# Stick-breaking attention with queries on partitions: the product of the stay probabilities by a VectorE scan, the weights turned back on TensorE

## The chip, the core and the metric

One core of one Trainium2 chip runs one launch of one decoder layer. Its engines work side by side and meet at semaphores: TensorE (PE for its matmuls, PEld for its weight loads), VectorE (DVE), ScalarE (ACT), GpSimd (POOL) and SyncE (SP, which here only issues DMAs). TensorE has a granted clock; a value of 1.00 in a row is 2.4 GHz, 0.50 is 1.2 GHz. The metric is the device time of the launch in microseconds (us). The median of the three runs shown of the kernel before is 673.02 us.

## What is computed

A sequence of 512 tokens of width 1024 goes through one input projection, eight attention heads of 64 dimensions beside a short gated convolution over 512 channels, an output projection with LayerNorm, and a mixture of 32 experts (two per token) with a second LayerNorm. All is float32. The part that matters here is the attention:

```python
z = jnp.einsum('bhqd,bhkd->bhqk', qb, kb) * scale
causal = s_pos[None, :] < t_pos[:, None]
log_stay = jnp.where(causal, jax.nn.log_sigmoid(-z), 0.0)
log_stay_after = lax.cumsum(log_stay, axis=3, reverse=True) - log_stay
a = jnp.where(causal, jnp.exp(jax.nn.log_sigmoid(z) + log_stay_after), 0.0)
outs.append(jnp.einsum('bhqk,bhkd->bhqd', a.astype(vb.dtype), vb))
```

For query t and key s the weight is sigmoid(z_ts), times the product of 1 - sigmoid(z_tj) over the keys j that lie between s and t. Since 1 - sigmoid(z) = sigmoid(-z), the sum of logs can as well be a running product.

## The kernel before

Every engine has its own hand-written list of instructions, and semaphores join the lists. The launch has these stages: adaLN vectors (`ada`, 24 chunks of 256 columns of w_ada, 8 before the projection and 16 beside what follows, each summed on DVE into `acc_rows`), the projection of q, k and v, the attention stage with the convolution in it, the row broadcasts (L1170), the output projection (L1180) with LayerNorm and router, then the 32 experts, in 16 pairs.

The attention stage works head by head. Of the 16 blocks of 128 queries by 128 keys, the 10 on and below the diagonal are kept, so that one head has ZW = 1280 score columns. They lie in three PSUM banks (`zbank(h)`, even and odd heads in different banks), with the keys on the 128 partitions:

- `scores(h)` on PE: 7 matmuls over the 128 rows of `kT`, which hold two heads; `qz` is q with the other head's 64 rows zeroed.
- `softplus_tail(h)` on ACT: Abs, Exp and Ln of the whole bank, then `softplus(h)` on DVE (L733), a mask of the diagonal blocks on POOL (L419), and `suffix_sums(h)` on DVE.
- `later_keys(h)` on PE (L1141): 8 matmuls with a triangle of -1 or with all -1 add the sums over later keys to the scores in PSUM, 1280 + 768 columns.
- Exp on ACT (L584) makes the weights, POOL masks them again, and `attend(p)` on PE (L1132) multiplies them with v, for two heads at a time, 64 output partitions each. `scores(h + 2)` may start only when the Exp has read the bank.

Between these, PE runs the 12 convolution projections `conv_proj(n)` (L1119, 8 matmuls of 512 columns each). They share one PSUM bank (bank 6), so each waits until ACT (`cc`) or DVE (`cx`, `cb`) has read the one before. CONV_AT spreads them over the heads. DVE does four more `ada` chunks (20 to 23) behind heads 0 to 3.

SP loads all weights in one fixed order through a ring of 4 buffers `stage` of 1 MB. A load is issued when the buffer's last user is done; for an ada chunk that is DVE's `ada`, for a convolution weight it is the second `conv_proj` that reads it. Two lines tie the stage to its end on PE:

```python
            pe.wait_ge(ada_done, NADACH - (ADA1 - ADA_PE))
            pe.wait_ge(prob_done, NH)
```

Of the kernel before, what the change touches and what calls it, by code (L numbers as in the profile page):

```python
# [80 lines left out]
CONV_AT = [0, 2, 3, 5, 6, 8, 9, 11, 12]  # L81
NOWHERE = 1024
OVT = 256
DIAG, OFF0, OFF2, OFF1, ZW = 0, 512, 896, 1024, 1280


def layer_kernel(nc, x, c, w_ada, b_ada, w_in, conv_w, w_out, ln1_g, ln1_b, w_router_group,
# [3 lines left out]
    with ctx:  # L91
# [6 lines left out]
        def sem(name):  # L98
# [12 lines left out]
        qz = at("qz", [P, NH, T], PAIR1)  # L111
        kT = at("kT", [P, NF, T], PAIR1 + 16 * KB)
        v = at("v", [P, TC, DA], PAIR1 + 24 * KB)
        expo = [at(f"expo{n}", [P, ZW], o) for n, o in enumerate(
            (PAIR1 + 32 * KB, PAIR1 + 37 * KB, REST + 48 * KB, PAIR1 + 42 * KB))]
        acc_cols = at("acc_cols", [P, ADA_PE * CW], PAIR1 + 32 * KB)
        conv_rows = at("conv_rows", [P, P], PAIR1 + 42 * KB)
        suffix = [at(f"suffix{n}", [P, 3 * P], REST + 53 * KB + n * 1536) for n in range(2)]
# [4 lines left out]
        softp = [at(f"softp{n}", [P, ZW], PAIR2 + 32 * KB + n * 5 * KB) for n in range(2)]  # L123
# [31 lines left out]
        tri_neg = sm("tri_neg", [P, P])  # L155
        neg_ones = sm("neg_ones", [P, P])
# [81 lines left out]
        z_done, abs_done, exp_done, ln_done = sem("z_done"), sem("abs_done"), sem("exp_done"), sem("ln_done")  # L238
        sp_done, sp_masked, suf_done, tri_done = sem("sp_done"), sem("sp_masked"), sem("suf_done"), sem("tri_done")
        prob_done, prob_masked, av_done, av_ev = sem("prob_done"), sem("prob_masked"), sem("av_done"), sem("av_ev")  # L240
# [153 lines left out]
        def _(pool):  # L394
# [5 lines left out]
            g.memset(neg_ones[:], -1.0).then_inc(fills, 1)  # L400
# [5 lines left out]
            pool.wait_ge(fills, 6)  # L406
# [3 lines left out]
            g.affine_select(out=tri_neg[:], in_=neg_ones[:], compare_op=ALU.is_ge, fill=0.0, base=0,  # L410
                            pattern=[[-1, P]], channel_multiplier=1)
            g.affine_select(out=before[:], in_=ones_b[:], compare_op=ALU.is_gt, fill=0.0, base=0,
                            pattern=[[1, P]], channel_multiplier=-1)
            g.memset(qz[:], 0.0).then_inc(consts, 1)

            def mask(t):

                d = t[:, DIAG:DIAG + T].rearrange("p (j t) -> p j t", t=P)
                return g.affine_select(out=d, in_=d, compare_op=ALU.is_gt, fill=0.0, base=0,  # L419
                                       pattern=[[0, TC], [1, P]], channel_multiplier=-1)  # L420

            def mask_probs(h):
                pool.wait_ge(prob_done, h + 1)
                mask(expo[h % 4]).then_inc(prob_masked, 1)

            for h in range(NH):
                pool.wait_ge(sp_done, h + 1)
                mask(softp[h % 2]).then_inc(sp_masked, 1)
                if h > 0:
                    mask_probs(h - 1)  # L430
            mask_probs(NH - 1)
# [89 lines left out]
        def _(act):  # L521
            s = nc.scalar
            s.preload_act_table_set("natural_log_exp_and_others")
# [6 lines left out]
            s.activation(csil[:, 1], csil[:, 0], ACT.Exp, scale=-1.0).then_inc(exp_c, 1)  # L530
# [9 lines left out]
            act.wait_ge(consts, 2)  # L540
            for n in range(16):
                act.wait_ge(proj_done, n + 1)
                src = ps[:, n % 4]
                if n < 4:
                    s.mul(qz[0:HD, 2 * n], src[0:HD], HD ** -0.5)
                    s.mul(qz[HD:P, 2 * n + 1], src[HD:P], HD ** -0.5).then_inc(proj_ev, 1)
                elif n < 8:
                    s.copy(kT[:, n - 4], src).then_inc(proj_ev, 1)
                else:
                    half, i = divmod(n - 8, TC)  # L550
                    s.copy(v[:, i, w_cols(half)], src[:, 0:CW]).then_inc(proj_ev, 1)

            def softplus_tail(h):

                e = expo[h % 4]
                act.wait_ge(z_done, h + 1)
                if h >= 4:
                    act.wait_ge(av_done, (h - 4) // 2 + 1)
                s.activation(e[:], zbank(h), ACT.Abs).then_inc(abs_done, 1)
                act.wait_ge(abs_done, h + 1)  # L560
# [790 lines left out]
```

## Time and profile before

| | |
|---|---|
| median of 3 runs | 673.02 us (667.49 to 673.24) |
| the profiled execution's span | 662.9 us |
| PE busy in it | 544.0 us (82%) |
| DVE busy | 268.7 us (41%) |
| ACT busy | 112.9 us (17%) |
| POOL busy | 107.8 us (16%) |
| mean granted TensorE clock | 0.923 |
| DMA | 164.11 MB, mean 248 GB/s |

The span runs from the first to the last instruction of one profiled execution; the device time of a run holds some us more around it. The busy shares are averages over stages that have different limits, so the stage that the change touches is to be read by itself. The profile's chain of waits follows the work that ended last back to what released it. PE stands in it with 67% of the span, DMA with 15%, and SP's queue, DVE, ACT and POOL with 6, 5, 2 and 2%.

### The profile page before, as it was taken

Reading aid. Unit: us, or ns where it says so; the run is one execution under the profiler, and the core shown is the slowest. Engines: PE = TensorE matmul, PEld = TensorE weight load, DVE = VectorE, ACT = ScalarE, POOL = GpSimd, SP = SyncE. Lnnn points to the kernel's source line nnn. Section 1 sums busy time; section 2 is a strip of 40 time slices with the busy share of each in tenths; the row PEclk is TensorE's granted clock in tenths of the full one; section 3 lists DMA queues with packets and bytes.
Section 4 is the critical chain, followed back from the end, with each engine's and each line's share of the span. In section 5 each row is a group of like instructions: output and inputs, shape, how many; then the busy total and the mean of one; then the engine's idle time right before and its main releaser. Section 6 shows DMA issues by size and latency. Waiting matters only on the chain.

```text
span 662.9 us, 6931 instructions
## 1 busy us (share of the span) xinstructions
PE 544.0 (82%) x2665; PEld 311.8 (47%) x2665; DVE 268.7 (41%) x508; ACT 112.9 (17%) x172; POOL 107.8 (16%) x97
## 2 busy tenths in 40 slices
PE   0999999998889998989998169999997868888400
PEld 0984447854455454544455135555553434445100
DVE  4646566641554032224564762232232222221295
ACT  0111110125313233130112012112111111111010
POOL 3000000000000000004354421112112010100156
PEclk9979999999999999999998569999999998888755
DMA  8990777653034500029805439999999999999353
GB/s 298 312 290 8 249 251 249 195 191 127 0 128 160 221 0 1 0 100 423 364 33 216 196 95 395 419 414 416 418 417 417 418 418 418 418 417 380 113 194 127
DMA packets 67011, 164.11 MB, mean 248 GB/s; under 512 B 7560, under 2 KB 44460, under 8 KB 58796
## 3 DMA queue, kind: packets, MB, share of 16 engines
q1 hardware_dynamic: 58416, 149.96, 59.5%
q0 software_dynamic: 4608, 8.40, 3.5%
q10 hardware_dynamic: 3964, 5.44, 2.4%
q8 instruction: 15, 0.25, 0.2%
q14 instruction: 8, 0.07, 0.0%
HBM read 159.58 MB, written 12.58 MB: 260 GB/s over the span
## 4 chain that ended last, share of the span: by engine, by line
PE 67%; DMA 15%; SPq 6%; DVE 5%; ACT 2%; POOL 2%; issue 1%; POOLq 1%; DVEq 0%
PE ps L1119 13%; DMA w_gu<-in_w_up_dram 11%; PE ps L1245 11%; PE ps L1088 9%; PE ps L1180 8%; PE ps L1254 5%; PE ps L1095 4%; SPq L317 4%; PE ps L1141 4%; PE ps L1046 3%; DMA stage<-in_w_ada_dram 2%; PE ps L1238 2%; SPq L321 2%; PE ps L1132 1%; PE ps L1105 1%; ACT expo L584 1%
## 5 line engine op out<-in xcount | busy, mean ns | idle before, releaser
L1245 PE MATMUL ps<-w_gu,xT 128*64 128x256 f32 x1024 | 128.4, 408 | 22.8 <-DMA w_gu<-in_w_up_dram 19.7
L1245 PEld LDWEIGHTS ps<-w_gu,xT 128*64 128x64 f32 x1024 | 76.7, 146 | 65.0 <-issue 16.8
L1119 PE MATMUL ps<-hT,stage 128*128 128x512 f32 x192 | 84.7, 594 | 3.3 <-DVE u_conv L754 1.8
L970 DVE TENSOR_TENSOR ysb<-ps,rows_gate 64x512 f32<-64x512 f32 x64 | 44.1, 689 | 52.3 <-PE ps L1254 51.9
L1254 PE MATMUL ps<-w_dn,hidT 128*64 128x512 f32 x256 | 61.3, 599 | 0.4 <-ACT hidT L626 0.4
L962 DVE TENSOR_TENSOR hid<-ps,silu_sb 128x128 f32<-128x128 f32 x32 | 9.3, 292 | 123.4 <-ACT silu_sb L632 123.4
L1119 PEld LDWEIGHTS ps<-hT,stage 128*128 128x128 f32 x192 | 36.1, 190 | 47.0 <-issue 46.7
L1088 PE MATMUL ps<-hT,stage 128*128 128x512 f32 x128 | 57.1, 609 | 1.1 <-DVE hT L723 1.1
L707 DVE SCALAR_TENSOR_TENSOR acc_rows<-stage,csil,acc_rows 128x256 f32<-128x256 f32 x112 | 54.3, 485 | 4.0
L1180 PE MATMUL ps<-wo,mixT 128*128 128x512 f32 x128 | 55.4, 592 | 0.0
L460 POOL DMA_INDIRECT y_dram<-ysb,slot_row x16 | 16.1, 1008 | 201.9 <-DVE ysb L970 201.9
L419 POOL TENSOR_SCALAR_AFFINE_SELECT softp<-softp 128x512 f32<-128x512 f32 x8 | 5.1, 637 | 254.1 <-DVE softp L733 254.1
L1088 PEld LDWEIGHTS ps<-hT,stage 128*128 128x128 f32 x128 | 25.0, 197 | 32.5 <-issue 31.4
L1180 PEld LDWEIGHTS ps<-wo,mixT 128*128 128x128 f32 x128 | 24.2, 190 | 29.7 <-issue 29.7
L632 ACT ACTIVATE silu_sb<-ps 128x128 f32<-128x128 f32 x32 | 8.9, 278 | 139.7 <-PE ps L1245 139.7
L1254 PEld LDWEIGHTS ps<-w_dn,hidT 128*64 128x64 f32 x256 | 17.1, 136 | 23.8 <-issue 20.9
L1095 PE MATMUL ps<-stage,hT 128*128 128x256 f32 x128 | 27.8, 379 | 0.0
L1046 PE MATMUL ps<-csil,stage 128*128 128x1 f32 x96 | 18.1, 319 | 11.7 <-DMA stage<-in_w_ada_dram 11.7
L1095 PEld LDWEIGHTS ps<-stage,hT 128*128 128x128 f32 x128 | 24.3, 190 | 3.7 <-issue 0.5
L733 DVE SCALAR_TENSOR_TENSOR softp<-ps,expo 128x1280 f32<-128x1280 f32 x8 | 11.9, 1486 | 33.7 <-ACT expo L563 33.7
L1046 PEld LDWEIGHTS ps<-csil,stage 128*128 128x128 f32 x96 | 18.2, 291 | 11.8 <-issue 11.8
L1238 PE MATMUL ps<-ident,xg 128*128 128x128 f32 x128 | 18.4, 289 | 5.7 <-DMA xg<-h_dram,slot_tok 5.7
(197 smaller groups left out, 558.0 us busy)
## 6 DMA issues: line engine op xcount, KB each, us to landing
w_gu<-in_w_gate_dram SPq DMA_DIRECT2D x32, 1024.0 KB, 20.4
w_gu<-in_w_up_dram SPq DMA_DIRECT2D x32, 1024.0 KB, 23.5
w_dn<-in_w_down_dram SPq DMA_DIRECT2D x32, 1024.0 KB, 24.0
stage<-in_w_ada_dram SPq DMA_DIRECT2D x24, 1024.0 KB, 8.0
stage<-in_w_in_dram SPq DMA_DIRECT2D x12, 1024.0 KB, 9.0
wo<-in_w_out_dram SPq DMA_DIRECT2D x1, 4096.0 KB, 17.4
y_tok<-y_dram SPq DMA_DIRECT2D x8, 512.0 KB, 7.5
xs<-in_x_dram ACTq DMA_DIRECT2D x1, 2048.0 KB, 14.0
```

What stands on the lines that cost most here:

```text
L317: sp.dma_start(w_gu[u][e][:, g], src).then_inc(ld_gu[u][e], 16)
L707: link(w.scalar_tensor_tensor(out=acc, in0=st[:, k], scalar=csil[:, 3, k:k + 1], in1=acc, op0=ALU.mult, op1=ALU.add))
L970: ins = w.tensor_tensor(ysb[u][e * HD:(e + 1) * HD, b * 512:(b + 1) * 512], ps[b * HD:(b + 1) * HD, 6 + e, :], gate2r[b * HD:(b + 1) * HD, ...
L1046: t.matmul(col, st[:, k, f * P:(f + 1) * P], csil[:, 3, k:k + 1], start=k == 0, stop=False)
L1088: ins = t.matmul(dst, st[:, k, f * P:(f + 1) * P], hT[:, k], start=k == 0, stop=k == KC - 1)
L1095: ins = t.matmul(dst[:, 0:CW], hT[:, k, i * P:(i + 1) * P], st[:, k], start=k == 0, stop=k == KC - 1)
L1119: ins = t.matmul(ps[:, 6], st[:, k, (f % 2) * P:(f % 2 + 1) * P], hT[:, k], start=k == 0, stop=k == KC - 1)
L1141: add = lambda to, m, r, stop=False: t.matmul(to, m, r, start=False, stop=stop, skip_group_check=True)
L1180: ins = t.matmul(ps[:, 4 + 2 * (i % 2) + n], mixT[:, k, i * P:(i + 1) * P], wo[:, k, n * 512:(n + 1) * 512], start=k == 0, stop=k == KC - 1)
L1238: ins = t.transpose(flat[:, k * P:(k + 1) * P], xg[u][:, k * P:(k + 1) * P], ident[:])
L1245: ins = t.matmul(ps[a * SLOTS:(a + 1) * SLOTS, 2 + e, 0:2 * P], xT[u][:, k, e * SLOTS:(e + 1) * SLOTS], w_gu[slot][e][:, :, k, a * P:(a + ...
L1254: ins = t.matmul(ps[b * SLOTS:(b + 1) * SLOTS, 6 + e, :], hidT[e][:, a * SLOTS:(a + 1) * SLOTS], w_dn[slot][e][:, a, b * 512:(b + 1) * 512 ...
```

## The change

The scores come out with the queries on the partitions. One `scores(p)` serves the two heads of a pair: for each query block, the 64 rows of one head in `qT` are the stationary operand and its 64 rows in `kT` the moving one, first for the even head (rows 0 to 63) and then for the odd one (rows 64 to 127), into different banks. ACT takes sigmoid(-z) into `stay` and sigmoid(z) into `prob`. POOL masks the diagonal blocks of both, each in two instructions. DVE runs one scan over `stay` from the last column to the first, a product which `block_end` (a bf16 row of zeros, with a one at the last key of each query block) sets back to 1, and multiplies `prob` by it. PE turns the 10 blocks of `prob` back with transposes (`turn_probs`) into the same banks, ACT copies them to `probT` (`probs_out`), and `attend(p)` needs 8 matmuls instead of 14. `later_keys`, the softplus and the suffix sums are gone. The convolution projections now stand three to a pair, and `ada(20 + p)` stands behind the third of each pair. ACT loads another table at the start and one more (for an Exp of 16 columns) ahead of the router's softmax.

```diff
-            def suffix_sums(h):
-                f, sx = softp[h % 2], suffix[h % 2]
...
+            def weights_of(h):
+                st = stay[h % 2]
+                dve.wait_ge(stay_masked, 2 * h + 2)
+                w.tensor_tensor_scan(out=st[:, 0:ZW][:, ::-1], data0=st[:, 0:ZW][:, ::-1], data1=block_end[:, ::-1],
+                                     initial=1.0, op0=ALU.mult, op1=ALU.max).then_inc(scan_done, 1)
+                dve.wait_ge(scan_done, h + 1)
+                dve.wait_ge(take_masked, 2 * h + 2)
+                w.tensor_tensor(prob[h % 2][:], prob[h % 2][:], st[:, 1:ZW + 1], ALU.mult).then_inc(prob_done, 1)
...
-            for h in range(NH):
-                softplus(h)
-                suffix_sums(h)
-                for n in range(CONV_AT[h], CONV_AT[h + 1]):
-                    conv(n)
-                if 20 + h < NADACH:
-                    ada(20 + h)
+            dve.wait_ge(consts, 8)
+            for p in range(NPH):
+                weights_of(2 * p)
+                conv(3 * p)
+                weights_of(2 * p + 1)
+                conv(3 * p + 1)
+                conv(3 * p + 2)
+                ada(20 + p)
...
+            def sigmoids(h):
+                act.wait_ge(z_done, h // 2 + 1)
+                if h >= 2:
+                    act.wait_ge(prob_done, h - 1)
+                s.activation(stay[h % 2][:, 0:ZW], zbank(h), ACT.Sigmoid, scale=-1.0).then_inc(stay_done, 1)
+                if h >= 2:
+                    act.wait_ge(probt_done, h - 1)
+                s.activation(prob[h % 2][:], zbank(h), ACT.Sigmoid).then_inc(take_done, 1)
...
+            def probs_out(h):
+                act.wait_ge(probt_done, h + 1)
+                if h >= 2:
+                    act.wait_ge(av_done, h // 2)
+                s.copy(probT[h % 2][:], zbank(h)).then_inc(probt_ev, 1)
...
+            for p in range(NPH):
+                sigmoids(2 * p)
+                sigmoids(2 * p + 1)
+                if p > 0:
+                    av_out(p - 1)
+                conv_cc(3 * p)
+                probs_out(2 * p)
+                conv_cc(3 * p + 1)
+                probs_out(2 * p + 1)
+                conv_cc(3 * p + 2)
+            av_out(NPH - 1)
...
+            def scores(p):
+                if p > 0:
+                    pe.wait_ge(probt_ev, 2 * p)
+                for i in (3, 2, 0, 1):
+                    for h in (2 * p, 2 * p + 1):
+                        b = (h % 2) * HD
+                        ins = t.matmul(zbank(h)[:, QROW[i]:QROW[i] + (i + 1) * P], qT[b:b + HD, p, i * P:(i + 1) * P],
+                                       kT[b:b + HD, p, 0:(i + 1) * P], start=True, stop=True, skip_group_check=True)
+                ins.then_inc(z_done, 1)
+
+            def turn_probs(h):
+                pe.wait_ge(prob_done, h + 1)
+                z, a = zbank(h), prob[h % 2]
                 for j in range(TC):
...
+                    for i in range(j, TC):
+                        ins = t.transpose(z[:, KROW[j] + (i - j) * P:KROW[j] + (i - j + 1) * P],
+                                          a[:, QROW[i] + j * P:QROW[i] + (j + 1) * P], ident[:])
+                ins.then_inc(probt_done, 1)
...
+            for p in range(NPH):
+                scores(p)
+                if p > 0:
+                    attend(p - 1)
+                conv_proj(3 * p)
+                turn_probs(2 * p)
+                conv_proj(3 * p + 1)
+                turn_probs(2 * p + 1)
+                conv_proj(3 * p + 2)
+            attend(NPH - 1)
...
             pe.wait_ge(ada_done, NADACH - (ADA1 - ADA_PE))
-            pe.wait_ge(prob_done, NH)
+            pe.wait_ge(probt_ev, NH)
```

On PE the kernel before has these rows for one head in the steady part of the stage, from the scores of a head over one convolution projection to the sums over later keys of the head before it (a name's number is a buffer; `x8` is eight such instructions):

```order
L1105 MATMUL ps<-qz,kT 128x128 x4
L1107 MATMUL ps<-qz,kT 128x384
L1108 MATMUL ps<-qz,kT 128x128
L1109 MATMUL ps<-qz,kT 128x256
L1119 MATMUL ps<-hT,stage_63 128x512 x8
L1141 MATMUL ps<-softp_81,tri_neg 128x512 x2
L1141 MATMUL ps<-softp_81,tri_neg 128x256
L1141 MATMUL ps<-softp_81,neg_ones 128x128
L1141 MATMUL ps<-suffix_76,neg_ones 128x256
L1141 MATMUL ps<-softp_81,neg_ones 128x128 x2
L1141 MATMUL ps<-suffix_76,neg_ones 128x128
```

The changed kernel has these for a whole pair of heads, with 8 `attend` matmuls (left out here) behind the scores:

```order
L1107 MATMUL ps<-kT,qT 128x512 x2
L1107 MATMUL ps<-kT,qT 128x384 x2
L1107 MATMUL ps<-kT,qT 128x128 x2
L1107 MATMUL ps<-kT,qT 128x256 x2
...
L1127 MATMUL ps<-hT,stage_61 128x512 x8
L1116 MATMUL ps<-ident,prob_79 128x128 x10
L1127 MATMUL ps<-hT,stage_63 128x512 x8
L1116 MATMUL ps<-ident,prob_80 128x128 x10
L1127 MATMUL ps<-hT,stage_63 128x512 x8
```

So every piece of attention work on PE now has a convolution projection on both sides, and nothing of it comes twice in a row but scores and `attend`.

On DVE the kernel before ends the stage like this (the last two heads, then the row work):

```order
L733 SCALAR_TENSOR_TENSOR softp_81<-ps,expo_72 128x1280
L740 TENSOR_TENSOR suffix_76<-softp_81 128x128
L741 TENSOR_TENSOR suffix_76<-softp_81 128x128
L743 TENSOR_TENSOR suffix_76<-softp_81,suffix_76 128x128
L762 TENSOR_TENSOR mixT<-ps,cc_sb_83 128x512
L778 TENSOR_SCALAR rows_a_91<-rows_a_91 128x1024
```

and the changed kernel like this (the scan is printed as a SCALAR_TENSOR_TENSOR at L740):

```order
L740 SCALAR_TENSOR_TENSOR stay_68<-stay_68,block_end 128x1280
L744 TENSOR_TENSOR prob_80<-prob_80,stay_68 128x1280
L763 TENSOR_TENSOR mixT<-ps,cc_sb_81 128x512
L763 TENSOR_TENSOR mixT<-ps,cc_sb_82 128x512
L713 TENSOR_SCALAR acc_rows<-stage_62,csil 128x256
L715 SCALAR_TENSOR_TENSOR acc_rows<-stage_62,csil,acc_rows 128x256 x7
L717 SCALAR_TENSOR_TENSOR acc_rows<-b_77,ident,acc_rows 128x256
L780 TENSOR_SCALAR rows_a_90<-rows_a_90 128x1024
```

The last `ada` chunk has moved from behind head 3 to the very end of the stage, behind the last convolution projection's reading.

## Rows read from the trace of the kernel before

**Rows 1.** Windows: busy us of each engine (instructions), granted clock, DMA share, GB/s.

```profile
core 0: us, PE busy (x) PEld busy (x) DVE busy (x) ACT busy (x) POOL busy (x), PEclk, DMA share, GB/s
133.50:288.00 154.50, 140.40 (x544) 77.32 (x544) 50.38 (x90) 43.83 (x40) 10.11 (x16) 1.00 0.26 89
288.00:389.00 101.00, 78.95 (x268) 42.93 (x268) 57.90 (x117) 15.52 (x21) 42.23 (x25) 0.85 0.58 226
```

**Rows 2.** Waits of PE from 133 to 289 us: total, times, longest.

```profile
PE ps L1105 <- ACT expo L584: 8.7, 6, 2.1
PE ps L1132 <- POOL expo L419: 2.0, 1, 2.0
PE ps L1119 <- DVE u_conv L754: 1.8, 2, 0.9
PE ps L1119 <- ACT cc_sb L577: 1.5, 2, 0.8
```

**Rows 3.** Chain of waits from 130 to 300 us: start, us, what.

```profile
136.04 0.89 PE ps L1105 x8
...
167.84 3.48 PE ps L1141 x16
171.35 1.25 ACT expo L584
172.64 1.16 PE ps L1105 x8
...
175.10 6.88 PE ps L1119 x16
...
189.95 2.32 PE ps L1132 x28
...
288.08 7.06 PE ps L1170 x16
```

**Rows 4.** Timeline of PE: start, us, line, operation, records [idle before].

```profile
135.88 1.05 PE L1105 MATMUL ps<-qz,kT 128*128 128x128 f32 x8
...
138.07 7.03 PE L1119 MATMUL ps<-hT,stage 128*128 128x512 f32 x16
```

**Rows 5.** Timeline of PE in the output projection.

```profile
338.76 1.07 PE L1190 MATMUL ps<-ident,h2p 128*128 128x128 f32 x8
339.67 0.59 PE L1180 MATMUL ps<-wo,mixT 128*128 128x512 f32 x1
```

**Rows 6.** Timeline of ACT.

```profile
175.14 1.24 ACT L559 ACTIVATE expo<-ps 128x1280 f32<-128x1280 f32 x1 [2.55 <-PE ps L1109]
```

**Rows 7.** Timeline of POOL.

```profile
213.22 0.64 POOL L419 TENSOR_SCALAR_AFFINE_SELECT softp<-softp 128x512 f32<-128x512 f32 x1 [15.19 <-DVE softp L733]
2.13 0.29 POOL L407 TENSOR_SCALAR_AFFINE_SELECT ident<-ident 128x128 f32<-128x128 f32 x1
```

**Rows 8.** Timeline of DVE.

```profile
182.01 0.69 DVE L754 TENSOR_TENSOR u_conv<-ps,cc_sb 128x512 f32<-128x512 f32 x1 [3.54 <-PE ps L1119]
...
184.04 0.75 DVE L759 SCALAR_TENSOR_TENSOR cc_sb<-u_conv,cwT,cc_sb 128x510 f32<-128x510 f32 x1
...
207.24 0.34 DVE L705 TENSOR_SCALAR acc_rows<-stage,csil 128x256 f32<-128x256 f32 x1
...
211.67 1.48 DVE L733 SCALAR_TENSOR_TENSOR softp<-ps,expo 128x1280 f32<-128x1280 f32 x1
...
297.22 1.22 DVE L781 TENSOR_TENSOR rows_a<-rows_a,g1r 128x1024 f32<-128x1024 f32 x1
```

**Rows 9.** The tile stage from 200 to 230 us (both landings fall here).

```profile
L311 SPq DMA_DIRECT2D stage<-in_w_in_dram x2: 373/478/582, 206.6 to 207.0; - x2
DMA to landing us min/median/max: 5.2/6.5/7.8
```

**Rows 10.** Windows, columns as in Rows 1.

```profile
40.00:42.00 2.00, 2.00 (x20) 2.00 (x20) 0.00 (x0) 0.00 (x0) 0.00 (x0) 1.00 1.10 348
42.00:44.00 2.00, 2.00 (x12) 2.00 (x11) 0.00 (x0) 0.00 (x0) 0.00 (x0) 0.52 1.10 349
286.00:288.00 2.00, 2.00 (x28) 1.34 (x22) 0.00 (x0) 0.00 (x0) 0.00 (x0) 1.00 0.00 0
```

More of the change, by code:

```diff
@@ L422, in mask_probs @@
-            def mask_probs(h):
-                pool.wait_ge(prob_done, h + 1)
-                mask(expo[h % 4]).then_inc(prob_masked, 1)
-            for h in range(NH):
[L427 to L431, printed above, removed]
+            g.memset(block_end[:], 0.0).then_inc(consts, 1)
+            pool.wait_ge(consts, 2)
+            for i in range(TC):
+                end = QROW[i] + (i + 1) * P
+                g.memset(block_end[:, end - 1:end], 1.0).then_inc(consts, 1)
@@ new lines, in _, with mask @@
+            for n in range(2):
+                g.memset(stay[n][:, ZW:ZW + 1], 1.0).then_inc(consts, 1)
+            def mask(t, fill, done):
+                d = t[:, P:ZW].rearrange("p (j t) -> p j t", t=3 * P)[:, :, 2 * P:]
+                g.affine_select(out=d, in_=d, compare_op=ALU.is_gt, fill=fill, base=0,
+                                pattern=[[0, 3], [-1, P]], channel_multiplier=1).then_inc(done, 1)
+                d = t[:, QROW[0]:QROW[0] + P]
+                g.affine_select(out=d, in_=d, compare_op=ALU.is_gt, fill=fill, base=0,
+                                pattern=[[-1, P]], channel_multiplier=1).then_inc(done, 1)
@@ L695, in _ @@
             dve.wait_ge(exp_c, 1)
-            link(w.tensor_scalar(csil[:, 2], csil[:, 1], 1.0, None, ALU.add))
-            link(w.reciprocal(csil[:, 1], csil[:, 2]))
             w.tensor_tensor(csil[:, 3], csil[:, 0], csil[:, 1], ALU.mult).then_inc(cs_ready, 1)
@@ L776, in _ @@
             dve.wait_ge(ld_b1, 16)
-            dve.wait_ge(tri_done, NH)
+            dve.wait_ge(probt_done, NH)
             link(w.tensor_scalar(a2r[:], a2r[:], 1.0, None, ALU.add))
@@ L1122, in attend @@
             def attend(p):
[L1124 removed]
+                pe.wait_ge(probt_ev, 2 * p + 2)
                 if p > 0:
                     pe.wait_ge(av_ev, p)
[L1127 to L1129 removed]
+                for j in range(TC):
@@ L1151, in _ @@
             pe.wait_ge(proj_ev, 16)
             pe.wait_ge(cw_ev, 1)
-            scores(0)
-            for h in range(NH):
-                if h + 1 < NH:
-                    scores(h + 1)
-                for n in range(CONV_AT[h], CONV_AT[h + 1]):
-                    conv_proj(n)
-                if h > 0 and h % 2 == 0:
-                    attend(h // 2 - 1)
-                later_keys(h)
-            attend(NH // 2 - 1)
+            for p in range(NPH):
[7 more added lines that the diff above has]
+                conv_proj(3 * p + 2)
```

126 lines of the change are left out of this document (32 added, 94 removed).

## The prediction

> **What bounds the kernel now.** I read the windows by stage first. The attention stage takes 154.5 us, and in it PE is busy for 140.4 us at a clock of 1.00, DVE for 50.4, ACT for 43.8 and POOL for 10.1, while DMA moves only 89 GB/s [rows 1]. PE is the limit, and what PE does or waits for is what the stage costs. Next I read PE's waits there. They make 14.0 us: 8.7 in six waits of `scores` for ACT's Exp, 2.0 of the last `attend` for POOL's mask, 3.3 of convolution projections for bank 6 [rows 2]. The chain of waits gives each piece its length. A convolution projection takes 6.88 us, `later_keys` 3.48, `attend` of two heads 2.32, the row broadcasts 7.06; the Exp of 1.25 lies bare between `later_keys` and `scores` [rows 3]. The scores of a head take 2.2 us, from their start at 135.88 to the projection at 138.07 [rows 4], and up to 2.46 behind a wait (172.64 to 175.10 [rows 3]); I use 2.3.
>
> What follows the stage starts from it. The row broadcasts at 288.08 [rows 3] need its end, and output projection, router and experts stand behind them. The prefetch of expert weights is issued behind the row broadcasts too. So a gain in the stage moves all that is left, and its last stages neither hide nor add.
>
> **PE's work, part by part.** (1) Convolution: 12 projections before and after, nothing changes.
>
> (2) `later_keys` goes: 8 x 3.48 = 27.8 us [rows 3].
>
> (3) The transposes come: 10 a head, 80 in all. Nearest row: 8 transposes of 128x128 from 338.76, the next matmul at 339.67 [rows 5], so 0.91 / 8 = 0.114 us each. Each leaves one record where a float32 matmul leaves two. 80 x 0.114 = 9.1 us. If they cost as much as matmuls of 128 columns (eight records in 0.89 us, so 0.22 for two [rows 3]), it is 17.8 us; I take 9.1, since it is the same operation with the same shape.
>
> (4) Scores. Before, 8 x 2.3 = 18.4 us. Now a pair has twice 1280 columns, each matmul over 64 rows, the two heads in turn in different row halves and banks. No row shows row halves. Lower bound: the halves run side by side, 2.3 us a pair, as column halves do in `attend`: two heads of 1280 columns each in 2.32 us [rows 3], which is the time of one head's 1280 columns of scores. Upper bound: one after the other, 4.6 us a pair and no gain. I take the lower, since `attend` is the nearest row: two independent matmuls of half the array. Four pairs make 9.2 us, 9.2 less than now.
>
> The Trainium skill, "TensorE: Matmul & The Clock Gate", section "Measured speedup vs the span model", gives 3.07 times for four row tiles, less than four. An estimate from it, 1.54 times for two, would be 3.0 us a pair and 2.8 us more in the sum. No run here shows it yet.
>
> (5) `attend`: 1280 columns a head as before, in 8 matmuls for 14. 2.3 us each, no change.
>
> PE's work falls by 27.8 - 9.1 + 9.2 = 27.9 us.
>
> **The waits.** All times now from the end E of a pair's third projection. DVE reads the bank (0.69) and, for a `cx`, does three more steps, 2.78 us in all (182.01 to 184.79), then `ada` takes 4.43 (207.24 to 211.67) [rows 8]. Meanwhile `scores` ends at E + 2.3; ACT makes four sigmoids of 1.24 [rows 6]; POOL masks each in two pieces, between 0.64 for all four blocks in one and 0.64 + 0.29 with a second one beside it [rows 7]. The first head's masks are done by about E + 6.
>
> The scan has no row. Lower bound: one pass of two operations over 1280 columns, 1.48 us at L733 [rows 8]. Upper bound: two such passes, 2.96, since each element must go through two operations before the next can start. I take 2.9. The product of two SBUF tiles: 1.22 for 1024 columns [rows 8], so 1.53 for 1280. `weights_of` is then 4.4 us. By the Trainium skill, "DVE: opcode table, instruction layouts, handler registers and perf-mode slots", section "Datapath and trigger behaviour", this scan runs at half throughput; no row shows that yet, and the sum would be the same within 0.5 us.
>
> - `turn_probs(2p)`: DVE has the weights at E + 0.1 + 2.8 + 4.4 + 4.4 = E + 11.7; PE arrives at E + 2.3 + 2.3 + 6.9 = E + 11.5. Wait 0.2 to 0.4 behind a `cx` (pairs 1 and 3), none behind a `cb` (pair 2). In pair 0, the chain is sigmoid, mask, scan, product, 6.9 us, against one projection of 6.9: about 0.1.
> - `turn_probs(2p + 1)`: PE comes 1.1 + 6.9 = 8.0 us after the end of the first projection, DVE needs 2.8 + 4.4 = 7.2. None.
> - The projections' bank: 0.7 of reading plus a handover is covered by transposes (1.1) or by scores and `attend`. The 3.3 us go.
> - `scores` of the next pair needs two copies of 1.24, under a projection of 6.9. The 8.7 us go, the 2.0 of the last `attend` too.
> - New: the row broadcasts wait for the last `ada`, now behind the last projection: 0.1 + 0.7 + 4.4 = 5.2 us, of which `attend` covers 2.3. Wait 3.0. Behind it stand the rows and all that follows.
> - Loads: the last convolution weight goes out when `ada(22)` is done, at E + 7.3 + 0.5 in pair 3, is wanted at E + 12.9, and lands in 5.2 us as the quicker of a pair, 7.8 as the slower [rows 9]. The big load of w_out is issued behind it. With 5.2 the wait is 0.1, with 7.8 it is 2.7; I take 0.2. Where this cover is gone, the wait counts in full.
>
> New waits: 3.0 + 0.8 + 0.2 + 0.1 = 4.1 against 14.0, a gain of 9.9. ACT per pair has 6 x 1.24 + 1.2 = 8.6 us, POOL under 4, DVE 2 x 4.4 + 3.5 + 4.4 = 16.7, all under PE's 27.5. The added table load stands in an idle ACT. On the start side, nothing of the stage's front moves: PE starts at 133.6 as before.
>
> **Sum.** 27.9 + 9.9 = 37.8 us, plus 1 us of small stalls at the pieces' borders that go with 64 fewer groups: 39. On the profiled execution 662.9 - 39 = 624 us of span; that execution stands 10.1 us under the median of the runs shown, so the median goes from 673.0 to **634 us**.
>
> **Rivals.**
> - *The row halves do not overlap.* Scores cost 4.6 a pair, 9.2 us more, and the waits of 0.8 vanish under it: 634 + 8.4 = 642. For it: no row shows row halves. Against: the column halves overlap fully.
> - *The weights come late.* A scan of 5 us (3.9 ns a column, 3.4 times L733's) makes `turn_probs(2p)` wait 2.5 behind a `cx`, 0.5 behind a `cb`, 2.2 in pair 0, and `turn_probs(2p + 1)` 1.2 behind a `cx`: 9 us more, 643. GpSimd masks held up by DVE, or the late convolution weight, would land at the same place with 1 to 4 us.
> - *DVE becomes the bound: slower.* With a scan of s us, DVE's work in a pair is 2s + 11; it decides above PE's 27.5, thus from s = 8.3 on, and adds 8 us for each further us of s over four pairs. At s = 8 some 30 us are lost, at 9.3 the whole gain; at 10.1 us (7.9 ns a column, the reversed order or the bf16 operand slowing each element) the time is 680. Against it: every float32 row of DVE here is near 1.2 ns a column [rows 8].
> - *The clock falls.* It fell to 0.52 at 42 us although PE was busy throughout, with matmuls of one column [rows 10]. The transposes are short too. But they are 1.1 us between projections of 6.9, and the stage stands at 1.00, also behind the wait of 2.0 [rows 2, 10]. If the 3.0 us before the row broadcasts brought it down, their 7.06 us [rows 3] would at most double: 641. Over the whole stage it would cost more than all that is won.
> - *Nothing changes*: some of PE's time would have to reappear elsewhere. With PE 91% busy in the stage I see no place.
>
> **From this to the numbers.** 634 (628 to 638): 0.62. Row halves in turn, 642: 0.18. Late weights, loads or clock ahead of the rows, 638 to 650: 0.12. DVE or clock as a new bound, slower: 0.03. A gain of under 1%: 0.02. A larger gain than 628: 0.03. The range that leaves out 2 in 10 at most is 626 to 646. A comparison of this kernel can tell about 1% from no change. Faster by over 1%: 0.95, within 1%: 0.02, slower: 0.03.
>
> **What would show each step.** In the profile after: the scores of a pair in 2.3 us (or 4.6); ten transposes in 1.15 us; one scan of 2.9 us; PE's waits for DVE ahead of transposes under 0.5 each; one wait of 3 us ahead of the row broadcasts, for `ada`; these starting near 249 us; a clock of 1.00 until there; the stages behind as long as before. A scan above 4 us, a clock of 0.50 in the stage, or an expert stage that is longer than before would make the forecast wrong.

## The result and the profile after

The changed kernel takes 629.61 us in the median (629.44 to 630.5, 4 runs) against 673.13 us of the kernel before on the same chip. The ratio is 0.9395, with a 95% interval of 0.9348 to 0.9441: 6% faster. Forecast were 634 us, between 626 and 646. Of the kernel before, one of 17 executions on a second chip took 3124.68 us for no known reason and is left out of every comparison below.

| | before | after |
|---|---|---|
| median | 673.13 us | 629.61 us |
| span of the profiled execution | 662.9 us | 627.7 us |
| PE busy | 544.0 us | 514.9 us |
| DVE busy | 268.7 us | 282.1 us |
| ACT busy | 112.9 us | 100.1 us |
| POOL busy | 107.8 us | 128.2 us |

The windows of the changed kernel, with the attention stage cut at 133.5 us as in [rows 1], and the engines in the same columns:

```profile
core 0: us, PE busy (x) PEld busy (x) DVE busy (x) ACT busy (x) POOL busy (x), PEclk, DMA share, GB/s
133.50:255.00 121.50, 116.47 (x410) 55.91 (x409) 68.35 (x75) 34.24 (x36) 33.13 (x32) 0.99 0.35 121
255.00:356.00 101.00, 78.71 (x272) 42.96 (x273) 60.17 (x123) 16.11 (x19) 42.49 (x25) 0.84 0.56 218
```

PE's waits in the changed kernel from 133 to 262 us (total, times, longest), the counterpart of [rows 2]:

```profile
PE ps L1162 <- DVE acc_rows L717: 2.9, 1, 2.9
PE ps L1116 <- DVE prob L744: 1.7, 3, 0.6
PE ps L1107 <- ACT v L554: 0.5, 1, 0.5
```

The 14.0 us of waits in [rows 2] are gone, and 4.6 new ones for DVE stand in their place; the 0.5 for ACT's `v`, ahead of the first scores, was there before as well. PE's timeline for one pair of the changed kernel, with the end of the stage (start, us, records, [idle before]):

```profile
160.64 2.43 PE L1107 MATMUL ps<-kT,qT 64*128 64x512 f32 x16
163.00 2.37 PE L1138 MATMUL ps<-probT,v 128*64 128x512 f32 x16
165.31 7.13 PE L1127 MATMUL ps<-hT,stage 128*128 128x512 f32 x16
173.01 1.31 PE L1116 MATMUL ps<-ident,prob 128*128 128x128 f32 x10 [0.57 <-DVE prob L744]
174.16 7.03 PE L1127 MATMUL ps<-hT,stage 128*128 128x512 f32 x16
181.03 1.25 PE L1116 MATMUL ps<-ident,prob 128*128 128x128 f32 x10
182.12 7.05 PE L1127 MATMUL ps<-hT,stage 128*128 128x512 f32 x16
...
250.48 8.83 PE L1162 MATMUL ps<-acc_rows,ones 128*128 128x512 f32 x16 [2.90 <-DVE acc_rows L717]
```

The reader is to see three things. A pair's scores occupy PE for 2.36 us (160.64 to 163.00), where each single head took as long before [rows 4]. Ten transposes take 1.09 us from start to start (181.03 to 182.12). And of the wait for DVE only 0.57 us shows, behind a first convolution projection.

From the first scores to the row broadcasts the stage now takes 115.9 us (134.55 to 250.48), before it took 154.4 (133.58 to 288.01). I call this the stage length below. It is the measure for the experiments, since the part in front of it varies from one execution to another: the first scores start between 133.58 and 138.00 us in the 13 traces below.

### The profile page after: what moved, and what is told of

It is laid out like the page before. It is cut to its first block, busy times and chain, and to the rows that moved or that the text cites. A ratio compares the mean times of both kernels' runs of the same rounds, so it can differ in the third digit from the quotient of the medians.

```text
span 627.7 us, 6651 instructions
## 1 busy us (share of the span) xinstructions
PE 514.9 (82%) x2521; PEld 287.7 (46%) x2521; DVE 282.1 (45%) x490; ACT 100.1 (16%) x161; POOL 128.2 (20%) x117
## 4 chain that ended last, share of the span: by engine, by line
PE 62%; DMA 16%; DVE 10%; SPq 6%; POOL 3%; issue 2%; ACT 1%; POOLq 1%; DVEq 0%
DMA w_gu<-in_w_up_dram 12%; PE ps L1237 12%; PE ps L1127 10%; PE ps L1090 9%; PE ps L1172 9%; PE ps L1246 5%; PE ps L1097 4%; SPq L320 4%; PE ps L1048 3%; DMA stage<-in_w_ada_dram 2%; DVE acc_rows L715 2%; SPq L324 2%; PE ps L1230 2%; PE ps L1116 1%; PE ps L1162 1%
## 5 line engine op out<-in xcount | busy, mean ns | idle before, releaser
L1237 PE MATMUL ps<-w_gu,xT 128*64 128x256 f32 x1024 | 126.2, 402 | 24.9 <-DMA w_gu<-in_w_up_dram 21.8
L426 POOL TENSOR_SCALAR_AFFINE_SELECT stay<-stay 128x384 f32<-128x384 f32 x8 | 5.3, 660 | 190.2 <-ACT stay L561 190.2
L1097 PE MATMUL ps<-stage,hT 128*128 128x256 f32 x128 | 27.8, 379 | 0.0
L740 DVE TENSOR_TENSOR_SCAN stay<-stay,block_end 128x1280 f32<-128x1280 f32 x8 | 24.1, 3015 | 4.7 <-POOL stay L429 4.7
```

What stands on the lines that cost most here:

```text
L740: w.tensor_tensor_scan(out=st[:, 0:ZW][:, ::-1], data0=st[:, 0:ZW][:, ::-1], data1=block_end[:, ::-1], initial=1.0, op0=ALU.mult, op1=ALU. ...
L1097: ins = t.matmul(dst[:, 0:CW], hT[:, k, i * P:(i + 1) * P], st[:, k], start=k == 0, stop=k == KC - 1)
L1237: ins = t.matmul(ps[a * SLOTS:(a + 1) * SLOTS, 2 + e, 0:2 * P], xT[u][:, k, e * SLOTS:(e + 1) * SLOTS], w_gu[slot][e][:, :, k, a * P:(a + ...
```

## The experiments

In same rows, scan from PSUM, no running product and two scans the attention weights are not the right ones, so that the router can send tokens to other experts. Of these only the stage is compared with the changed kernel; their times are given for completeness. The stage lengths:

| kernel | first scores | row broadcasts | stage, us | waits of PE for DVE in it, us |
|---|---|---|---|---|
| before | 133.58 | 288.01 | 154.4 | 1.8 |
| before, once more | 137.34 | 293.44 | 156.1 | 1.8 |
| before, reordered | 136.62 | 280.75 | 144.1 | 1.7 |
| changed | 134.55 | 250.48 | 115.9 | 1.7 + 2.9 |
| changed, once more | 137.12 | 253.07 | 115.9 | 1.7 + 2.9 |
| ada early (two executions) | 136.11, 137.05 | 247.53, 248.48 | 111.4, 111.4 | 0.5 |
| same rows | 134.32 | 257.32 | 123.0 | 0.5 + 2.9 |
| heads apart | 133.84 | 254.65 | 120.8 | 0.5 + 2.9 |
| scan from PSUM | 135.61 | 250.27 | 114.7 | 0.5 + 2.9 |
| no running product | 138.00 | 252.06 | 114.1 | 0 + 2.9 |
| two scans | 134.42 | 263.68 | 129.3 | 11.1 + 2.9 |
| turned by matmuls | 133.84 | 258.98 | 125.1 | 1.6 + 2.9 |

### Row halves: both heads in the same rows

```diff
-                        b = (h % 2) * HD
+                        b = 0
```

> Both heads of a pair take their scores from rows 0 to 63, so the odd heads' scores are those of the even head, and the two no longer lie in different row halves. Number and size of all instructions are the same. Theory (the row halves run side by side, and that halves the scores): the 16 records of a pair go from 2.4 us to 4.6 to 4.7, the stage grows by 4 x 2.3 = 9.2, less the 1.1 of waits for VectorE that vanish under it: 8 us more than the changed kernel, 637 to 638. Rival: a matmul over 64 rows is cheaper by itself, then the time stays at 630.

Measured: 635.67 us (two runs). The scores and what follows them, from PE's timeline of this kernel:

```profile
162.56 4.58 PE L1107 MATMUL ps<-kT,qT 64*128 64x512 f32 x16
167.07 2.38 PE L1138 MATMUL ps<-probT,v 128*64 128x512 f32 x16
```

The same 16 records take 4.51 us from start to start instead of 2.36. A matmul over 64 rows is not cheaper by itself; two that lie in different halves run side by side. The stage grows by 7.1: 4 x 2.15 = 8.6 more work, less the 1.1 us of waits for DVE in pairs 1 and 3 that PE no longer has, and some tenths at the borders. The factor is 4.51 / 2.36 = 1.91. The Trainium skill, "TensorE: Matmul & The Clock Gate", section "Measured speedup vs the span model", has 3.07 for four row tiles; the forecast's estimate from it, 1.54 for two, is too low here.

### Row halves: one head after the other

```diff
-                for i in (3, 2, 0, 1):
-                    for h in (2 * p, 2 * p + 1):
+                for h in (2 * p, 2 * p + 1):
+                    for i in (3, 2, 0, 1):
```

> The four score matmuls of the even head come first and then the four of the odd head, instead of in turn; the row halves and all sizes stay. Theory (two neighbours in the queue must lie in different halves to overlap): only the last of the even head and the first of the odd one overlap, a pair's scores take 2.43 + about 1.7 to 2.2 us, close to the 4.58 of both heads in one half, and the stage grows by 6 to 8 us. Rival (the engine looks far enough ahead for the other half's work): 2.4 us a pair and no change.

Measured: 632.72 us (two runs), stage 120.8. The rows of PE's timeline that answer to those above:

```profile
161.53 4.04 PE L1107 MATMUL ps<-kT,qT 64*128 64x512 f32 x16
165.50 2.37 PE L1138 MATMUL ps<-probT,v 128*64 128x512 f32 x16
```

3.97 us, near the 4.51 of one half alone: the rival, that the engine finds the other half's work further back in its queue, falls. The overlap comes from the order "even head, odd head" of equal pieces; the 0.54 us saved fit the one place where the halves meet. The stage grew by 4.9 rather than 6 to 8, because 1.61 x 4 = 6.4 us more of PE's work swallowed the 1.1 us of waits again.

### The transposes: ordinary matmuls in their place

```diff
-                        ins = t.transpose(z[:, KROW[j] + (i - j) * P:KROW[j] + (i - j + 1) * P],
-                                          a[:, QROW[i] + j * P:QROW[i] + (j + 1) * P], ident[:])
+                        ins = t.matmul(z[:, KROW[j] + (i - j) * P:KROW[j] + (i - j + 1) * P],
+                                          a[:, QROW[i] + j * P:QROW[i] + (j + 1) * P], ident[:],
+                                       start=True, stop=True, skip_group_check=True)
```

> The changed kernel with the blocks turned by ordinary float32 matmuls against the identity instead of transposes: same operands, same 80 places, two records each instead of one. This puts a number on the forecast's upper bound for that term. Theory (a transpose takes half of such a matmul): ten of them go from 1.09 us to 2.2, 80 add 8.9, and some of the 1.1 of waits for VectorE is taken up by it: 8 to 9 us more than the changed kernel in the attention stage (124 to 125 for 115.9), about 638 us. Rival (the transposes are bound by the weight loads): under 2 us.

Measured: 637.44 us (two runs), stage 125.1, 9.2 more. From PE's timeline:

```profile
183.82 2.39 PE L1116 MATMUL ps<-ident,prob 128*128 128x128 f32 x20
186.05 7.03 PE L1128 MATMUL ps<-hT,stage 128*128 128x512 f32 x16
```

Ten take 2.23 us against 1.09. The 80 transposes thus cost 80 x 0.109 = 8.7 us, and the form of the instruction is worth as much again. The waits for DVE did not shrink (1.6): the transposes stand behind DVE's product, so their own length cannot hide it.

### The scan: its running product left out

```diff
-                w.tensor_tensor_scan(out=st[:, 0:ZW][:, ::-1], data0=st[:, 0:ZW][:, ::-1], data1=block_end[:, ::-1],
-                                     initial=1.0, op0=ALU.mult, op1=ALU.max).then_inc(scan_done, 1)
+                w.scalar_tensor_tensor(out=st[:, 0:ZW][:, ::-1], in0=st[:, 0:ZW][:, ::-1], scalar=1.0, in1=block_end[:, ::-1],
+                                       op0=ALU.mult, op1=ALU.max).then_inc(scan_done, 1)
```

> The scan is replaced by one elementwise pass with the same operations, tiles and order (multiply by 1, then maximum), so the running product is left out. Theory (a scan costs two passes): 1.5 us instead of 2.8 to 3.1; the waits ahead of transposes in pairs 0, 1 and 3 (1.7 us in all) go, and the time falls by 1 to 2 us, to 628 or 629; the wait of 2.9 ahead of the row broadcasts stays. Rival (the reversed order or the bf16 operand makes it slow): it still takes near 2.8 us, and nothing changes.

The time of this run, 930.5 us, says nothing on the stage: its other weights send the tokens to other experts, and more expert blocks are run (1536 records of the gate and up matmuls for 1024). The stage is 114.1 us, 1.9 less than the changed kernel's. DVE's timeline in the changed kernel, in an undisturbed place:

```profile
175.56 2.82 DVE L740 TENSOR_TENSOR_SCAN stay<-stay,block_end 128x1280 f32<-128x1280 f32 x1
178.42 1.49 DVE L744 TENSOR_TENSOR prob<-prob,stay 128x1280 f32<-128x1280 f32 x1
```

and without the running product:

```profile
177.88 1.49 DVE L740 SCALAR_TENSOR_TENSOR stay<-stay,block_end 128x1280 f32<-128x1280 f32 x1
179.41 1.49 DVE L744 TENSOR_TENSOR prob<-prob,stay 128x1280 f32<-128x1280 f32 x1
```

The same tiles, types and reversed order take 1.49 without the dependence from column to column and 2.82 with it. It is also what DVE's pass L733 took in the kernel before, forward and in float32 (1.48 [rows 8]), so the reversed order and the bf16 operand cost nothing in such a pass. The factor of 1.9 agrees with the half throughput that the Trainium skill states for this scan ("DVE: opcode table, instruction layouts, handler registers and perf-mode slots", section "Datapath and trigger behaviour").

### The scan, and GpSimd beside it

The changed kernel's masks on POOL are of two kinds. In its timeline:

```profile
138.40 0.52 POOL L426 TENSOR_SCALAR_AFFINE_SELECT stay<-stay 128x384 f32<-128x384 f32 x1 [134.43 <-ACT stay L561]
138.88 0.30 POOL L429 TENSOR_SCALAR_AFFINE_SELECT stay<-stay 128x128 f32<-128x128 f32 x1
139.46 2.99 POOL L426 TENSOR_SCALAR_AFFINE_SELECT prob<-prob 128x384 f32<-128x384 f32 x1 [0.28 <-ACT prob L564]
```

while DVE does this:

```profile
139.31 2.82 DVE L740 TENSOR_TENSOR_SCAN stay<-stay,block_end 128x1280 f32<-128x1280 f32 x1 [4.30 <-POOL stay L429]
142.80 1.72 DVE L744 TENSOR_TENSOR prob<-prob,stay 128x1280 f32<-128x1280 f32 x1 [0.67 <-POOL prob L429]
```

The mask that began 0.15 us after the scan ended only behind it, and DVE's product then waited 0.67 us for POOL's second mask. The next kernel gives the scan one SBUF input less:

```diff
+                dve.wait_ge(take_done, h + 1)
-                w.tensor_tensor_scan(out=st[:, 0:ZW][:, ::-1], data0=st[:, 0:ZW][:, ::-1], data1=block_end[:, ::-1],
+                w.tensor_tensor_scan(out=st[:, 0:ZW][:, ::-1], data0=zbank(h)[:, ::-1], data1=block_end[:, ::-1],
```

> The scan takes its first operand from the scores in PSUM instead of from the masked stay tile, so the result is not the product wanted; it reads one SBUF tensor instead of two, and waits also for the second sigmoid (take_done), since ScalarE reads that bank. Theory (GpSimd's masks stood still because a VectorE instruction with two SBUF inputs keeps it out of SBUF): a mask that takes 2.8 to 3.0 us beside a scan in the changed kernel (0.52 or 0.30 when alone) takes no more than 0.8 beside this scan, while those beside the product, which still has two SBUF inputs, stay at 1.5; the scan itself still takes about 2.8. The time changes by under 1 us either way. Rival (a mask is slow for another reason, as ScalarE's writes): masks beside the scan stay near 2.8.

Measured: 626.74 us (two runs). POOL and DVE in the same place of the stage:

```profile
140.52 0.52 POOL L426 TENSOR_SCALAR_AFFINE_SELECT prob<-prob 128x384 f32<-128x384 f32 x1 [0.28 <-ACT prob L564]
140.99 0.29 POOL L429 TENSOR_SCALAR_AFFINE_SELECT prob<-prob 128x128 f32<-128x128 f32 x1
```

```profile
140.58 2.82 DVE L741 TENSOR_TENSOR_SCAN stay<-ps,block_end 128x1280 f32<-128x1280 f32 x1 [4.44 <-ACT prob L564]
143.44 1.49 DVE L745 TENSOR_TENSOR prob<-prob,stay 128x1280 f32<-128x1280 f32 x1
```

The scan still takes 2.82, and the mask beside it 0.52 instead of 2.99. ACT's writes are the same as before, so that rival falls. The kernel without the running product fits too: its first pass of 1.49 us held the mask for 1.73. In these traces a VectorE instruction with two SBUF inputs holds a mask on GpSimd until it ends, and the scan with a single SBUF input does not. The Trainium skill names contention on the two engines' shared SBUF interfaces for VectorE instructions with two SBUF inputs ("GPSIMD Engine Reference", section "1. Specifications"), and the trace agrees (2.99 against 0.52). It works the other way as well: in the changed kernel five of the eight scans took 3.12 or 3.14 us, those that began while a mask was running, and with one SBUF input all eight took 2.81 or 2.82. The part on masks beside the product was not tested: none fell beside it there. The price in this kernel is small: with the masks free the stage is 1.3 us shorter, the wait of 0.53 in pair 0 is gone, and those of 0.57 in pairs 1 and 3 are 0.25. The expectation of a time within 1 us was missed, since 626.74 is 2.9 under the changed kernel's 629.61. The stage accounts for 1.3 of it, and the clock, which did not fall ahead of the row broadcasts here, for 1.7.

### DVE's order: `ada` ahead of the third reading

```diff
                 conv(3 * p + 1)
-                conv(3 * p + 2)
                 ada(20 + p)
+                conv(3 * p + 2)
```

> The changed kernel with one move on VectorE: ada(20 + p) stands ahead of conv(3p + 2) instead of behind it, so that its 4.4 us lie under the third convolution projection of the pair (6.9 us). Theory (the waits that are left hang on VectorE's order): the wait of 2.90 us ahead of the row broadcasts goes; with it the clock stays at 1.00 and the broadcasts take 7.06 us again instead of 8.83; the two waits of 0.57 ahead of transposes in pairs 1 and 3 go too. Together 2.9 + 1.8 + 1.1 = 5.8 us less than the changed kernel, about 624 us. Rival: the clock falls for another reason (the transposes, say), then only 4.0 us are won and the broadcasts still take 8.8. Rival: the ada chunk's load is late there, then VectorE waits for a stage buffer and the third projection's reading comes late.

> The kernel with ada(20 + p) ahead of conv(3p + 2), against the changed kernel on the same chip. From the trace of its first run its stage is 4.5 us shorter (111.4 for 115.9), and the row broadcasts 1.7 shorter where the clock would have fallen. Expected 4 to 6 us less than the changed kernel in the median.

Measured: 625.15 us (623.93 to 626.76, 4 runs) the first time. On the second chip it took 623.16 us (621.66 to 624.83, 6 runs), beside 629.48 us of the changed kernel there; their ratios to the kernel before are 0.9288 (0.9255 to 0.9320) and 0.9393 (0.9348 to 0.9438). Of PE's waits in the stage this is left:

```profile
PE ps L1116 <- DVE prob L744: 0.5, 1, 0.5
PE ps L1107 <- ACT v L554: 0.5, 1, 0.5
```

The wait of 2.9 us and both of 0.57 are gone, 4.0 us in all, and the stage is 4.5 us shorter in both executions; the medians differ by 6.3, a little more than the 4 to 6 expected. The first rival of the expectation, a clock that falls for another reason, did not show: the broadcasts took 7.1 us both times. The loads were not late: no wait for a stage buffer appears. This version beats both kernels.

### The clock ahead of the row broadcasts

> The changed kernel, unaltered, on the same chip and beside the same runs of the kernel before as the next three. It gives the base for them, and whether the front part and the clock ahead of the row broadcasts vary from one execution to the next. Theory (only the moment differs): the attention stage, from the first scores to the row broadcasts, takes 115.9 us again; the broadcasts take 7.1 (clock held) or 8.8 (clock fallen). Rival (a fixed property of the program): 8.8 each time.

Measured: 629.48 us (628.74 to 631.99, 4 runs). The stage is 115.9 us again, and the same wait stands ahead of the row broadcasts, but these take less than in the first execution:

```profile
253.07 7.13 PE L1162 MATMUL ps<-acc_rows,ones 128*128 128x512 f32 x16 [2.91 <-DVE acc_rows L717]
```

Windows of 2 us of the first execution show where its 8.83 came from (columns as above, the granted clock is third from the end):

```profile
248.00:250.00 2.00, 0.00 (x0) 0.00 (x0) 1.86 (x5) 0.21 (x1) 0.00 (x0) 1.00 0.46 152
250.00:252.00 2.00, 1.52 (x3) 0.71 (x4) 0.43 (x1) 0.30 (x1) 0.00 (x0) 0.89 0.86 346
252.00:254.00 2.00, 2.00 (x4) 0.78 (x3) 0.00 (x0) 0.87 (x2) 0.00 (x0) 0.50 0.07 27
254.00:256.00 2.00, 2.00 (x5) 0.92 (x4) 0.00 (x0) 0.67 (x2) 0.00 (x0) 0.76 0.00 0
```

The granted clock fell to 0.50 (1.2 GHz) right behind the wait. The rival, a fixed property of the program, falls. With the same wait of 2.90 or 2.91 the broadcasts took 8.8 us in the changed kernel, in same rows, in no running product, in two scans and in turned by matmuls, and 7.1 in its second execution, in scan from PSUM and in heads apart: five of eight. In both executions of ada early, without the wait, 7.1. The wait thus costs 2.9 us, and 1.7 more in a good half of the executions. What decides between them was not found.

### Two scans: where VectorE's time starts to show

```diff
+                link(w.tensor_tensor_scan(out=st[:, 0:ZW][:, ::-1], data0=st[:, 0:ZW][:, ::-1], data1=block_end[:, ::-1],
+                                          initial=1.0, op0=ALU.mult, op1=ALU.max))
                 w.tensor_tensor_scan(out=st[:, 0:ZW][:, ::-1], data0=st[:, 0:ZW][:, ::-1], data1=block_end[:, ::-1],
```

> The scan is done twice, the second over the result of the first, so the weights are wrong. This doubles the cost that the forecast had to bound, to 6.1 us a head, and tests the forecast's account of what is hidden. Theory (VectorE's list decides when transposes start): waits ahead of transposes of 3.3 in pair 0, 3.6 and 2.3 in pairs 1 and 3, 1.6 in pair 2, together 15 us more in the attention stage than the changed kernel (131 us). Rival (slack elsewhere takes it up): under 8 us. Rival (VectorE becomes the bound, 2 x 6.1 x 4 more): 24 us. The parts behind the attention stage depend on the data through the router and are not compared.

Measured: 644.75 us (two runs, 641.68 and 647.82), stage 129.3 us, 13.3 more, near the 15 of the theory and far from both rivals. PE's timeline at the place where a term failed:

```profile
178.26 1.31 PE L1118 MATMUL ps<-ident,prob 128*128 128x128 f32 x10 [3.43 <-DVE prob L746]
179.40 8.73 PE L1129 MATMUL ps<-hT,stage 128*128 128x512 f32 x16
188.07 1.31 PE L1118 MATMUL ps<-ident,prob 128*128 128x128 f32 x10
...
209.17 1.31 PE L1118 MATMUL ps<-ident,prob 128*128 128x128 f32 x10 [1.20 <-DVE prob L746]
```

The waits of 3.05, 3.43, 1.20 and 3.43 are there as worked out (3.3, 3.6, 1.6, 3.6). The two of 2.3 at the second transposes of pairs 1 and 3 are not. First, two undisturbed scans are 5.7 us and not 6.1. Secondly, behind each wait of 3.43 the clock fell to 0.50, as in this window of 2 us:

```profile
180.00:182.00 2.00, 2.00 (x4) 0.90 (x3) 1.96 (x3) 0.83 (x1) 0.00 (x0) 0.50 0.00 0
```

The next projection took 8.73 us in pair 1. In pair 3 the ten transposes took 1.68 from start to start (1.15 behind other waits) and the projection 8.18 (7.03 elsewhere). PE thus arrived 1.8 us later both times, and found the weights ready. So of the 13.3 us some 9.4 are waits and 3.6 a slower TensorE.

### The kernel before: an execution more

> The kernel before, unaltered, profiled once more. Its first profiled execution had a span of 662.9 us while the medians of its runs lay between 668 and 673; the changed kernel's span and times differ by only 1.9. Theory (the kernel before has a part whose length varies, outside the attention stage): its attention stage is again 154.5 us, and the rest differs by some us in a stage to be named. Rival (the attention stage itself varies): it differs there, and the gain of the change is larger than one pair of traces shows.

Measured: 668.12 us (664.59 to 673.74, 10 runs); the profiled execution took 669.37 us with a span of 667.5, so the time lies 1.9 above the span. That is the same distance as in the changed kernel (629.51 and 627.7). The difference of 4.6 us to the first trace has its places. The first scores start at 137.34 instead of 133.58, 3.8 us later. Inside the stage the clock fell once, behind the wait of 2.07:

```profile
158.00:160.00 2.00, 2.00 (x14) 1.66 (x12) 0.00 (x0) 1.94 (x3) 0.00 (x0) 1.00 0.91 297
160.00:162.00 2.00, 0.21 (x2) 0.01 (x1) 0.87 (x1) 2.00 (x2) 0.00 (x0) 1.00 1.10 364
162.00:164.00 2.00, 1.72 (x9) 1.72 (x10) 1.26 (x3) 0.23 (x1) 1.23 (x2) 0.70 1.09 346
164.00:166.00 2.00, 2.00 (x6) 1.30 (x6) 0.56 (x3) 0.00 (x0) 0.00 (x0) 0.50 0.12 35
```

which makes the stage 1.7 us longer. The rest is 0.8 us shorter. So both answers of the expectation hold in part, and the first trace of the kernel before was of a quick execution: its 662.9 and 1.9 make 664.8, less than any of the four times behind the median of 673.13.

### The kernel before with another order on TensorE

```diff
             for h in range(NH):
+                for n in range(CONV_AT[h], CONV_AT[h + 1]):
+                    conv_proj(n)
                 if h + 1 < NH:
                     scores(h + 1)
-                for n in range(CONV_AT[h], CONV_AT[h + 1]):
-                    conv_proj(n)
```

> The kernel before, where only TensorE's order changes: in head h the convolution projections now come ahead of scores(h + 1) instead of behind it, so that later_keys(h - 1) and scores(h + 1), which waits for the Exp between them, have a projection between them. It asks how much of the gain needs the new arithmetic and how much was order. Theory (the six waits of 8.7 us for the Exp come from the order alone): they go, no other takes their place, since the softplus chain of a head (about 7 us) then lies under later_keys and a projection (10.4); the stage takes about 146 us for 154.5, and the time falls by 8 to 9 us against the kernel before. Rival (the softplus chain becomes late ahead of later_keys): waits for the suffix sums on VectorE take the place of the old ones.

Measured: 656.37 us (654.78 to 657.67, 4 runs), ratio to the kernel before 0.9827 (0.9793 to 0.9861), 1.7% faster. PE's waits from 130 to 290 us:

```profile
PE ps L1132 <- POOL expo L419: 2.0, 1, 2.0
PE ps L1119 <- DVE u_conv L754: 1.7, 2, 0.9
PE ps L1119 <- ACT cc_sb L577: 1.5, 2, 0.8
PE ps L1105 <- ACT v L551: 0.5, 1, 0.5
```

The 8.7 us for the Exp [rows 2] are gone and nothing came in their place; the stage is 144.1 us, 10.3 less. The other 1.6 stand at the same six borders: from the start of a `later_keys` to the projection behind the next scores PE's timeline has 7.26 us in the kernel before (167.68 to 174.94), 1.33 of them wait, and 5.67 for the same two pieces here (166.18 to 171.85). A bare wait cost 0.27 us more than its own length. About a quarter of what the change won in the stage (10.3 of 38.5) could be had without new arithmetic, by a projection between `later_keys` and the scores that wait for its bank.

## Why the prediction was right, point by point

- **What bounds the stage**: PE, as said. Everything that changed PE's work or waits moved the stage by about that, and where a wait was free to shrink it did.
- **`later_keys` for transposes**: 27.8 us out, and 80 transposes in at 0.109 us (0.114 forecast); the upper bound of 0.22 is what matmuls cost there.
- **Scores in row halves**: the lower bound was right, 2.36 us a pair (2.3 forecast), shown from both sides by same rows and heads apart. The nearest row, `attend` in its column halves [rows 3], was a better guide than the estimate of 1.54. The 2.46 read for scores behind a wait came from the chain; PE's timeline has 2.30 there (172.64 to 174.94), the value that was used.
- **The scan**: 2.82 to 3.14 us against 2.9 taken, near the upper of the two bounds. The longer ones lie above that bound (2.96), for the masks beside them, which the forecast did not count.
- **The waits**: forecast 3.0 + 0.8 + 0.2 + 0.1, found 2.9 + 1.1 + 0 + 0.5. Two small terms were off. The chain of pair 0 was given 6.9 us and no contention; POOL's second mask stood still behind the scan, and the wait became 0.53. In pairs 1 and 3 it is 0.57, since the scan there took 3.14 and `ada` some tenths more, while POOL was masking beside them; with the scan at 2.81 (scan from PSUM) these two waits were 0.25. POOL, put at under 4 us a pair, was busy for 33.1 in the four, which delayed PE nowhere else. The load of the last convolution weight was in time.
- **The stage as a whole**: 38.5 us shorter against 39 forecast. Of these 28.0 are work (27.8 less 8.7 for the transposes, plus 8.9 from the scores), 9.4 waits, and 1.1 are left for the borders of the pieces, which the forecast had put at 1.
- **The step that failed** is the last one, from the span to the time. The forecast took the profiled execution as standing 10.1 us under the median and carried this distance over. But a run's time lies only 1.9 us above its span, in both kernels; the other 8.2 were that this one execution of the kernel before was quicker than the median. The second trace, with a span 4.6 us longer, places 3.8 of them in the front part and 1.7 in the stage, less 0.8 elsewhere; what the slower executions at the median spend more is not in any trace. So the span was forecast at 624 and came out at 627.7, 3.7 too low, while the median was forecast at 634 and came out at 629.6, 4.4 too high. That the second miss is not larger is partly luck: the 8.2 us too many were in part made up by the 3.7 too few. With the right distance the forecast would have been 626 us.
- **The spans and the medians**: the 35.2 us between the two spans are 38.5 of the stage, less 1.0 of a later start of the scores (134.55 for 133.58), 2.0 from the row broadcasts to the experts (1.7 of them the clock) and 0.3 behind. By the medians of the first chip the gain is 43.5 us, 5 more than the stage of these two traces shows. On the second chip the changed kernel (629.48) is 38.6 us under the ten executions of "an execution more" (668.12), and 41.2 under the 16 others there (670.6). The kernel before ranges from 664.59 to 673.74 us in those ten alone, the changed one from 628.74 to 631.99 in four. How much of the 5 us is gain, and how much the choice of executions, is open. A fall of the clock in the stage of the kernel before explains 1.7 in one of its executions; its seven exposed waits for the Exp and the mask may give it more occasions for that than the changed kernel has, which was not measured.
- **The rivals**: that the halves do not overlap, fell. Late weights: the price for a scan of 5 us was not run, but two scans (5.7) put 13.3 us on the stage, with four of the six waits where the account has them. DVE as the bound: not reached even at two scans. (The rows beside that rival are 1.2 to 1.5 ns a column, the short ones more than the 1.2 named.) The clock: it fell where the forecast had said it might, ahead of the row broadcasts, and cost 1.7 us and not the upper 7. The forecast's ground for trusting it in the stage, that it had stood behind a wait of 2.0, was one execution: in the second one of the same kernel it fell behind 2.07.

## What to carry to other kernels

When the bounding engine has fill work (here 12 projections of 6.9 us), put one piece of it between every two steps of a chain that go through other engines; this alone was worth 10 us in the kernel before. Here float32 matmuls over 64 rows paid off in full only with neighbours in the queue in different halves, piece by piece in turn (2.36 us a pair, 3.97 with the heads apart). And read several executions of the kernel before, not one, before turning a difference of spans into a difference of times.

## What the runs showed of the hardware

- The same 2.9 us of idle PE was followed by a fall of the clock to 1.2 GHz in five of eight executions and by none in three; once (in the kernel before) it fell behind 2.07 us, in another execution of that kernel it did not; in two scans it fell behind both waits of 3.43 and not behind that of 3.05. Each fall cost 1.7 or 1.8 us.
- A GpSimd mask of 0.52 us takes as long as the VectorE instruction that runs beside it when this one has two SBUF inputs (2.99 beside a scan of 2.82, 1.73 beside a pass of 1.49), and 0.52 beside a scan that has one. The scan is held up too: 3.12 or 3.14 instead of 2.82 when a mask was running at its start.
- A running product along 1280 columns costs 2.82 us and the same pass without the dependence 1.49; reversed and with a bf16 second operand, that pass takes what a forward float32 one did (1.48).
- Float32 matmuls of 64 rows in alternate row halves ran side by side: 16 records in 2.36 us, 4.51 in one half. A float32 transpose of 128x128 took 0.109 us in a row of ten, the same block by a matmul against the identity 0.223.
